# The expert stage of a decoder kernel: another order of the experts' work, two pairs of down operands, single tiles for gathered tokens and expert outputs, all subtractions on VectorE

## The chip, the core and the metric

One core of a Trainium2 chip runs the whole kernel. The metric is the device time of an execution in microseconds (us). A span is the time from the first to the last instruction of the one profiled execution.

## What is computed

One inference step of a hybrid decoder layer: 1024 prompt tokens and 32 sample tokens go through a projection, an mLSTM branch and a sliding-window attention branch, a merge, and then a mixture of experts. The part that matters here is the last:

```python
def expert(args):
    xb, e = args
    return (jax.nn.silu(xb @ w_gate_e[e]) * (xb @ w_up_e[e])) @ w_down_e[e]

ys = lax.map(expert, (xs, blk_e)).reshape(rows, d)
out = jnp.zeros((n_tok + 1, d), jnp.float32).at[row_tok].add(ys.astype(jnp.float32) * row_w[:, None])
```

There are 32 experts (`NE`), each with gate and up matrices of 1024 x 256 and a down matrix of 256 x 1024 in fp32, 1 MB each. Every one of the 1056 tokens goes to two experts of one group, so an expert sees 66 tokens on average. A block holds up to 128.

## The kernel before

Products are made in three matmuls of float32r operands: each fp32 operand is split into a high part (a copy that rounds, on ScalarE) and a low part (operand minus high part, a subtraction), and `three` (L782) adds low x high, high x low and high x high. So each weight matrix costs a 1 MB load, a ScalarE copy of 128 x 2048 and a subtraction of 128 x 2048.

The expert stage runs all 32 experts in a pipeline written out by hand; each engine has its own loop over `e`, and semaphores join them. Per expert:

- SP (L726 to L736) loads the gate, up and down matrices into five raw tiles in turn (`raw`, two of them called `stage`), in the order of `ORDER` (L537). A load waits until the low part of the matrix five places earlier has been made.
- GpSimd (L2486 to L2504) gathers the expert's rows with an indirect DMA into `xg`, two tiles in turn (`gather`, L2470), makes the low part of the up matrix (`low`, L2481), and scatters the expert's result from `yo`, two tiles in turn (`store_y`, L2476). The gather of expert e+2 waits for the transposes of expert e.
- ScalarE (L1632 to L1656) makes the high parts of the weights (`main_high`), of the transposed x (`x_high`) and of h (`h_high`), the sigmoid (`silu`), and copies the result out of PSUM (`y_out`).
- VectorE (L2328 to L2340) makes the low parts of the gate and down matrices, of x (`x_low`) and of h (`h_low`), and the hidden product (`hidden`).
- TensorE (L1274 to L1287) runs in turn: `gate_up(e)` (24 matmuls of 512 columns), the two transposes of h of expert e-1, the eight transposes of x of expert e+1, and `down(e-1)` (12 matmuls).

Gate and up operands have two sets of tiles (`GUH`, `GUL`, by parity of e). The down operand has one pair (`dh`, `dl`), so the high part of the next down matrix waits until `down` of the expert before is done. `idx` holds, for each expert, the rows to gather and the rows to write; rows beyond an expert's count point out of bounds and are skipped. A loop for experts with more than 128 rows stands behind the stage; it isn't entered with these inputs.

Ahead of the stage, routing is computed; behind it, a last stage waits for all stores (`m_end`), loads the scattered results and adds them to the residual.

Of the kernel before, what the change touches and what calls it, by code (L numbers as in the profile page):

```python
# [15 lines left out]
F32R = mybir.dt.float32r  # L16
# [7 lines left out]
D = 1024  # L24
# [47 lines left out]
def build(nc, x_prompt, x_sample, state_C, state_n, state_m, cache_k, cache_v, w_in, b_if, norm_mix,  # L72
# [28 lines left out]
    with ctx:  # L101
# [145 lines left out]
        with s4:  # L247
# [19 lines left out]
                OB = r4("OB", [128, 2 * NT, 2, NBLK])  # L267
            gu1h = a4("gu1h", [128, 2 * CHUNK], F32R)
            gu1l = a4("gu1l", [128, 2 * CHUNK], F32R)
            dh = a4("dh", [128, CHUNK], F32R)  # L270
            dl = a4("dl", [128, CHUNK], F32R)
            raw = stage + [a4(f"raw{i}", [128, CHUNK]) for i in range(2)]
            a4("padw", [128, HOLE - 8 * CHUNK])
            idx = a4("idx", [128, 2, NBLK], I32)
            wgt = a4("wgt", [128, 2, NT])
            ovt = a4("ovt", [1, 2, NOVER], I32)
# [27 lines left out]
            s4b = ExitStack()  # L304
            with s4b:
                c4 = lambda n, s, dt=F32: alloc(s4b, n, s, dt)
                xg = [c4(f"xg{i}", [128, D]) for i in range(2)]
                xh = [c4(f"xh{i}", [128, KT, 128], F32R) for i in range(2)]
                xl = [c4(f"xl{i}", [128, KT, 128], F32R) for i in range(2)]
                ixs = c4("ixs", [128, 1], I32)  # L310
                dxs = c4("dxs", [128, 1], I32)
                sg_ = c4("sg_", [128, FF])
                hh = c4("hh", [128, FF])
                hTh = c4("hTh", [128, 2, 128], F32R)
                hTl = c4("hTl", [128, 2, 128], F32R)
                yo = [c4(f"yo{i}", [128, D]) for i in range(2)]
            s4c = ExitStack()
            with s4c:
                d4 = lambda n, s, dt=F32: alloc(s4c, n, s, dt)
# [1 line left out]
        gE = raw[3][:, 0:D]  # L321

        GUH, GUL = [whi2[:, :], gu1h[:, :]], [wlo2[:, :], gu1l[:, :]]


        pb = [ctx.enter_context(nc.psum_tensor(f"pb{i}", [128, 512], F32)) for i in range(4)]
# [209 lines left out]

        ORDER = [("g", 0), ("u", 0), ("g", 1)]  # L537
        for e_ in range(NE + 1):
            ORDER += [(m, k) for m, k in (("u", e_ + 1), ("d", e_ - 1), ("g", e_ + 2)) if 0 <= k < NE
                      and (m, k) not in ORDER]  # L540
        PLACE = {c: q for q, c in enumerate(ORDER)}
        NRAW = len(raw)
        HI, LO = {"g": g_hi, "u": u_hi, "d": d_hi}, {"g": g_lo, "u": u_lo, "d": d_lo}
# [10 lines left out]
        def half(tiles, par, m):  # L554

            if m == "d":
                return tiles[2].rearrange("p (k n) -> p k n", k=2)
            return tiles[par].rearrange("p (k n) -> p k n", k=KT)[:, :, (m == "u") * FF:(1 + (m == "u")) * FF]

        WHI, WLO = GUH + [dh[:, :]], GUL + [dl[:, :]]  # L560

        R_END = 4

# [213 lines left out]
        def _(pe):  # L777
# [4 lines left out]
            def three(out, lh, ll, rh, rl, first, last):  # L782

                pe.matmul(out, ll, rh, start=first, stop=False)  # L784
                pe.matmul(out, lh, rl, start=False, stop=False)  # L785
                return pe.matmul(out, lh, rh, start=False, stop=last)  # L786
# [458 lines left out]
            def transposes_h(e):  # L1245
                pe.wait_ge(e_hh, e + 1)
                for k in range(2):
                    mm = pe.transpose(pb[0][:, k * 128:(k + 1) * 128], hh[:, k:FF:2], ident)
                mm.then_inc(e_ht, 1)
# [9 lines left out]
                               k == 0, k == KT - 1)  # L1259
                mm.then_inc(e_gu, 1)  # L1260

            def down(e):
                pe.wait_ge(e_lo, e + 1)
                pe.wait_ge(d_lo, e + 1)
                for k in range(2):
                    for n_ in range(2):
                        wsl = slice(k * D + n_ * 512, k * D + (n_ + 1) * 512)
                        mm = three(pq[:, n_, :], hTh[:, k, :], hTl[:, k, :], dh[:, wsl], dl[:, wsl], k == 0, k == 1)
                mm.then_inc(e_y, 1)

            transposes_x(0, 0, 16)
            for e in range(NE + 1):
                if e < NE:
                    if e >= 2:  # L1274
                        pe.wait_ge(e_hh, e - 1)
                    gate_up(e, e % 2)
                if e >= 1:
                    if e >= 2:
                        pe.wait_ge(e_lo, e - 1)
                    transposes_h(e - 1)  # L1280
                if e + 1 < NE:
                    pe.wait_ge(e_xl, e + 1)
                    transposes_x(e + 1, (e + 1) % 2, 16 * ((e + 1) // 2 + 1))
                if e >= 1:
                    if e >= 2:
                        pe.wait_ge(e_yc, e - 1)
                    down(e - 1)  # L1287
            any_ = pe.value_load(ovt[0:1, 0, 0:1], min_val=0, max_val=1)
            with pe.If(any_ > 0):
                with pe.Fori(0, NOVER) as j:  # L1290
                    used_ = pe.value_load(ovt[0:1, 0, bass.ds(j, 1)], min_val=0, max_val=1)
                    with pe.If(used_ > 0):
                        e = j + NE
                        pe.wait_ge(e_xl, e)
                        transposes_x(e, 0, j * 16 + 16 * (NE // 2 + 1))
                        pe.wait_ge(e_hh, e)
                        gate_up(e, 0)
                        pe.wait_ge(e_lo, e)
                        transposes_h(e)
                        pe.wait_ge(e_yc, e)  # L1300
                        down(e)
                    with pe.Else():
                        pe.nop()
            with pe.Else():
# [5 lines left out]
        def _(act):  # L1310
# [289 lines left out]
            def main_high(m, e):  # L1600
                q = PLACE[m, e]
                high(q, m, e % 2, landed(q))
# [23 lines left out]

            def y_out(e, par, stored):
                act.wait_ge(e_y, e + 1)
                act.wait_ge(st_y[par], stored)
                copy(yo[par][:, :].rearrange("p (a n) -> p a n", a=2), pq[:, :, :]).then_inc(e_yc, 1)  # L1630

            act.wait_ge(r_v, R_END)  # L1632
            x_high(0, 0)
            main_high("g", 1)
            for e in range(NE + 2):
                if e + 1 < NE:
                    if e >= 1:
                        act.wait_ge(e_gu, e)
                    main_high("u", e + 1)
                if 1 <= e <= NE:  # L1640
                    if e >= 2:
                        act.wait_ge(e_y, e - 1)
                    main_high("d", e - 1)
                if e >= 2:
                    y_out(e - 2, e % 2, 16 * ((e - 2) // 2 + 1))
                if 1 <= e <= NE:
                    h_high(e - 1)
                if e < NE:
                    if e >= 1:
                        act.wait_ge(e_hh, e)  # L1650
                    silu(e, e % 2)
                if e + 1 < NE:
                    x_high(e + 1, (e + 1) % 2)
                if e + 2 < NE:
                    act.wait_ge(e_gu, e + 1)
                    main_high("g", e + 2)  # L1656
            any_ = act.value_load(ovt[0:1, 0, 0:1], min_val=0, max_val=1)
            with act.If(any_ > 0):
                with act.Fori(0, NOVER) as j:
                    used_ = act.value_load(ovt[0:1, 0, bass.ds(j, 1)], min_val=0, max_val=1)  # L1660
                    with act.If(used_ > 0):
                        e = j + NE
                        act.wait_ge(e_gu, e)
                        act.wait_ge(e_y, e)
                        for i, m in enumerate("gud"):
                            high(i, m, 0, j * 16 + (LAST[i] + 16))
                        x_high(e, 0)
                        silu(e, 0)
                        h_high(e)
                        y_out(e, 0, j * 16 + 16 * (NE // 2 + 1))  # L1670
                    with act.Else():
                        act.nop()
            with act.Else():
# [12 lines left out]
        def _(ve):  # L1686
# [640 lines left out]

            x_low(0, 0)  # L2328
            for e in range(NE + 1):
                if e + 1 < NE:  # L2330
                    low(PLACE["g", e + 1], "g", (e + 1) % 2, e + 1)
                if e >= 1:
                    low(PLACE["d", e - 1], "d", 0, e - 1)
                    h_low(e - 1)
                if e < NE:
                    if e >= 1:
                        ve.wait_ge(e_ht, e)
                    hidden(e, e % 2)
                if e + 1 < NE:
                    x_low(e + 1, (e + 1) % 2)  # L2340
            any_ = ve.value_load(ovt[0:1, 0, 0:1], min_val=0, max_val=1)
            with ve.If(any_ > 0):
                with ve.Fori(0, NOVER) as j:
# [38 lines left out]
        def _(gp):  # L2382
# [105 lines left out]
            gp.wait_ge(r_v, R_END)  # L2488
            for i in range(2):
                gp.wait_ge(st_h[i], 16 * ((NT + 1 - i) // 2))  # L2490
            for x in xg:
                gp.memset(x[:, :], 0.0)
            gp.drain()
            gather(idx[:, 0, 0:1], 0)
            gather(idx[:, 0, 1:2], 1)
            for e in range(NE + 2):
                if e + 2 < NE:
                    gp.wait_ge(e_xt, e + 1)
                    gather(idx[:, 0, e + 2:e + 3], e % 2)
                if e + 1 < NE:  # L2500
                    low("u", e + 1)
                if e >= 2:
                    gp.wait_ge(e_yc, e - 1)
                    store_y(idx[:, 1, e - 2:e - 1], e % 2)  # L2504
# [103 lines left out]
```

## Time and profile before

| | us |
|---|---|
| median of 3 runs | 1966.74 (1950.81 to 1970.0) |
| the profiled execution's own time | 1960.17 |
| its span | 1958.4 |
| first transpose of x to landing of the last store | 1533.9 to 1912.0 |
| one period of the settled expert stage | 11.2 |

In the rows further down, PE is TensorE's matmuls, DVE is VectorE, ACT ScalarE, POOL GpSimd. A group is named by its line, engine and operation, and by the tiles it writes and reads; buffer numbers are left out. Line L1318 is the helper that ScalarE's copies share, L2305 is VectorE's weight subtraction, L2483 GpSimd's, L2472 the gather, L2477 the store. L784 to L786 are the three matmuls, L1242 the transposes of x, L1248 those of h. `gu1h`, `whi` and `gu1l`, `wlo` are the high and low gate and up operands of the two parities. What stands in brackets is the idle time just before the instruction and what ended it.

### The profile page before, as it was taken

To read this page: it belongs to the slowest core of one execution; us is meant where nothing else is said; L and a number is where in the kernel's file an instruction comes from. 1 tells how busy PE (TensorE), PEld (TensorE's weight loads), DVE (VectorE), ACT (ScalarE), POOL (GpSimd) and SP (SyncE) were. 2 spreads that over 40 slices of the span, in tenths; PEclk is the share of its full clock that TensorE was granted. 3 is DMA by queue.
4 is the path that set the end of the run, shared out by engine and by line. 5 is a ranking of instruction groups with operands and counts; after the bars stand their busy time and mean duration, and the time that the engine had idled before them with its cause. 6 is when DMAs were issued, how large, how long until landed. Compare 5 with 4: busy or idle time off the path is not lost.

```text
span 1958.4 us, 27717 instructions
## 1 busy us (share of the span) xinstructions
PE 1697.9 (87%) x11221; PEld 1539.7 (79%) x11222; DVE 911.7 (47%) x1527; ACT 695.9 (36%) x1248; POOL 429.2 (22%) x241
## 2 busy tenths in 40 slices
PE   5969899999998999999999669998993688888870
PEld 4958898998987999888888459998993577767760
DVE  5433113123122001565566352344226498998957
ACT  4312222232221221433434231322022477677642
POOL 3000101002002000000000140000022487887842
PEclk7979999999998999999999679999996799999995
DMA  5033714508417222433321253435123499999946
GB/s 182 1 108 63 123 39 90 112 22 99 125 21 130 85 88 92 138 117 106 100 75 63 105 207 88 121 99 179 39 88 114 145 325 329 333 327 334 330 149 270
DMA packets 147568, 272.16 MB, mean 139 GB/s; under 512 B 44124, under 2 KB 114076, under 8 KB 134060
## 3 DMA queue, kind: packets, MB, share of 16 engines
q1 hardware_dynamic: 111792, 210.76, 33.2%
q0 software_dynamic: 16736, 40.14, 6.4%
q10 hardware_dynamic: 18912, 19.47, 5.9%
q8 instruction: 90, 1.47, 0.4%
q14 instruction: 38, 0.31, 0.1%
HBM read 223.22 MB, written 65.38 MB: 147 GB/s over the span
## 4 chain that ended last, share of the span: by engine, by line
PE 72%; DVE 10%; ACT 6%; issue 5%; DMA 3%; DVEq 2%; POOL 1%; SPq 0%; POOLq 0%; ACTq 0%
PE pb L784 14%; PE pb L785 13%; PE pb L786 13%; PE pb L1003 8%; DVE dl L2305 4%; ACT gu1h L1318 2%; PE pw L784 2%; PE pw L785 2%; PE pw L786 2%; ACT dh L1318 2%; PE pw L1014 2%; PE pw L892 1%; PE pq L858 1%; PE pb L1025 1%; PE pq L784 1%
## 5 line engine op out<-in xcount | busy, mean ns | idle before, releaser
L784 PE MATMUL pb<-whi,aTl 128*128 128x256 f32 (+1 forms) x1296 | 377.7, 291 | 17.1 <-ACT zo L1318 8.8
L785 PE MATMUL pb<-wlo,aTh 128*128 128x256 f32 (+1 forms) x1296 | 369.1, 285 | 0.0
L786 PE MATMUL pb<-whi,aTh 128*128 128x256 f32 (+1 forms) x1296 | 366.5, 283 | 0.0
L784 PEld LDWEIGHTS pb<-whi,aTl 128*128 128x128 f32 (+1 forms) x1296 | 236.1, 182 | 28.6 <-ACT zo L1318 13.0
L784 PE MATMUL pb<-aTh,wlo 128*128 128x352 f32 x720 | 235.9, 328 | 20.6 <-DVE mixT L2067 8.7
L786 PEld LDWEIGHTS pb<-whi,aTh 128*128 128x128 f32 (+1 forms) x1296 | 237.3, 183 | 1.0
L785 PEld LDWEIGHTS pb<-wlo,aTh 128*128 128x128 f32 (+1 forms) x1296 | 236.0, 182 | 2.1
L785 PE MATMUL pb<-aTl,whi 128*128 128x352 f32 x720 | 232.7, 323 | 0.0
L786 PE MATMUL pb<-aTh,whi 128*128 128x352 f32 x720 | 232.6, 323 | 0.0
L1694 DVE TENSOR_TENSOR wlo<-stage,whi 128x2048 fp32r<-128x2048 f32 x34 | 77.8, 2288 | 225.8 <-ACT whi L1318 225.8
L1318 ACT ACTIVATE whi<-stage 128x2048 fp32r<-128x2048 f32 (+1 forms) x80 | 109.8, 1397 | 132.0 <-PEq L1203 47.7
L784 PEld LDWEIGHTS pb<-aTh,wlo 128*128 128x128 f32 x720 | 136.8, 190 | 24.9 <-issue 15.8
L785 PEld LDWEIGHTS pb<-aTl,whi 128*128 128x128 f32 x720 | 137.1, 190 | 0.0
L786 PEld LDWEIGHTS pb<-aTh,whi 128*128 128x128 f32 x720 | 136.6, 190 | 0.0
L1003 PE MATMUL pb<-aTh,wlo 128*128 128x352 f32 x384 | 126.4, 329 | 0.3 <-PE pb L786 0.3
L1003 PE MATMUL pb<-aTh,whi 128*128 128x352 f32 x384 | 126.1, 328 | 0.0
L1003 PE MATMUL pb<-aTl,whi 128*128 128x352 f32 x384 | 124.3, 324 | 0.0
L1318 ACT ACTIVATE zo<-pb 128x256 f32<-128x256 f32 (+1 forms) x90 | 34.5, 383 | 224.0 <-PE pb L786 213.4
L2305 DVE TENSOR_TENSOR dl<-raw,dh 128x2048 fp32r<-128x2048 f32 x19 | 103.2, 5434 | 21.5 <-ACT dh L1318 21.5
L2431 POOL DMA_DIRECT2D oT_scratch<-ot x16 | 12.0, 753 | 455.7 <-ACT ot L1318 455.7
L1471 ACT ACTIVATE Sm<-Sm,nmx 128x256 f32<-128x256 f32 x128 | 63.5, 497 | 114.4 <-DVE nmx L1958 114.4
L784 PE MATMUL pq<-dh,hTl 128*128 128x512 f32 x128 | 54.2, 423 | 47.7 <-DVE hTl L2325 46.7
(411 smaller groups left out, 3446.5 us busy)
## 6 DMA issues: line engine op xcount, KB each, us to landing
stage<-in_w_in SPq DMA_DIRECT2D x30, 1024.0 KB, 5.6
raw<-in_w_gate_e SPq DMA_DIRECT2D x19, 1024.0 KB, 6.8
raw<-in_w_up_e SPq DMA_DIRECT2D x19, 1024.0 KB, 8.8
raw<-in_w_down_e SPq DMA_DIRECT2D x19, 1024.0 KB, 7.8
stage<-in_w_gate_e SPq DMA_DIRECT2D x13, 1024.0 KB, 6.9
stage<-in_w_up_e SPq DMA_DIRECT2D x13, 1024.0 KB, 8.7
stage<-in_w_down_e SPq DMA_DIRECT2D x13, 1024.0 KB, 8.2
zt_scratch<-zo ACTq DMA_DIRECT2D x80, 128.0 KB, 2.4
```

Of the source, the lines that this page charges most:

```text
L784: pe.matmul(out, ll, rh, start=first, stop=False)
L785: pe.matmul(out, lh, rl, start=False, stop=False)
L786: return pe.matmul(out, lh, rh, start=False, stop=last)
L858: mm = pe.matmul(pq[0:n, 1, 0:MD + 1], qT[:, d, tok(c)], Ce[:, d, :], start=(d == 0), stop=(d == 1))
L892: mm = pe.matmul(pw[:, d, 0:MD + 1], kw[c % 2][:, d * 128:(d + 1) * 128], v1[:, c, :], start=True, stop=True)
L1003: mm = pe.matmul(ZB[f % 2][:, 0:NC], lh, rh, start=(k == 0 and m == 0), stop=(k == KT - 1 and m == 2))
L1014: mm = pe.matmul(pw[:, e, v * 256:(v + 1) * 256], qTs[lo:lo + AD, gp * 4 + 2 * (p % 2) + v, :], kTs[lo:lo + AD, gp, :], start=True, stop=True)
L1025: mm = pe.transpose(AB[v][:, (2 * e + half) * 128:(2 * e + half + 1) * 128], Sm[p % 2][:, 2 * e + v, half * 128:(half + 1) * 128], ident)
L1318: return act.activation(out, in_, ACT.Copy, scale=scale)
L1471: act.activation(x, x, ACT.Exp, bias=nmx[:, h:h + 1], accum_out=den[:, h:h + 1])
L1694: ve.tensor_tensor(wlo[sl], stage[st][:, :], whi[sl].bitcast(F32), ALU.subtract).then_inc(w_lo, 1)
L2305: ve.tensor_tensor(half(WLO, par, m), rawv(q, m), half(WHI, par, m).bitcast(F32), ALU.subtract).then_inc(LO[m], 1)
```

## The change

The diff, cut to its core (a second, unentered loop for overfull experts is adapted in the same way):

```diff
-            dh = a4("dh", [128, CHUNK], F32R)
-            dl = a4("dl", [128, CHUNK], F32R)
+            d0h = a4("d0h", [128, CHUNK], F32R)
+            d0l = a4("d0l", [128, CHUNK], F32R)
...
-            a4("padw", [128, HOLE - 8 * CHUNK])
+            sg_ = a4("sg_", [128, FF])
+            hh = a4("hh", [128, FF])
...
-                xg = [c4(f"xg{i}", [128, D]) for i in range(2)]
+                xg = [c4("xg", [128, D])] * 2
...
-                yo = [c4(f"yo{i}", [128, D]) for i in range(2)]
+                yo = [c4("yo", [128, D])] * 2
+                d1h = c4("d1h", [128, CHUNK], F32R)
+                d1l = c4("d1l", [128, CHUNK], F32R)
...
-            ORDER += [(m, k) for m, k in (("u", e_ + 1), ("d", e_ - 1), ("g", e_ + 2)) if 0 <= k < NE
-                      and (m, k) not in ORDER]
+            ORDER += [(m, k) for m, k in (("u", e_ + 1), ("d", e_), ("g", e_ + 2)) if 0 <= k < NE]
...
             for e in range(NE + 1):
+                if e + 1 < NE:
+                    pe.wait_ge(e_xl, e + 1)
+                    transposes_x(e + 1, (e + 1) % 2, 16 * ((e + 1) // 2 + 1))
                 if e < NE:
                     if e >= 2:
                         pe.wait_ge(e_hh, e - 1)
                     gate_up(e, e % 2)
                 if e >= 1:
                     if e >= 2:
-                        pe.wait_ge(e_lo, e - 1)
-                    transposes_h(e - 1)
-                if e + 1 < NE:
-                    pe.wait_ge(e_xl, e + 1)
-                    transposes_x(e + 1, (e + 1) % 2, 16 * ((e + 1) // 2 + 1))
-                if e >= 1:
-                    if e >= 2:
                         pe.wait_ge(e_yc, e - 1)
-                    down(e - 1)
+                    down(e - 1, (e - 1) % 2)
+                if e < NE:
+                    if e >= 1:
+                        pe.wait_ge(e_lo, e)
+                    transposes_h(e)
...
                 act.wait_ge(e_y, e + 1)
-                act.wait_ge(st_y[par], stored)
+                act.wait_ge(st_y[1 - par], stored)
...
             for e in range(NE + 2):
+                if 1 <= e <= NE:
+                    if e >= 2:
+                        act.wait_ge(e_y, e - 1)
+                    h_high(e - 1)
+                if e >= 2:
+                    y_out(e - 2, e % 2, 16 * ((e - 1) // 2 + 1))
                 if e + 1 < NE:
                     if e >= 1:
                         act.wait_ge(e_gu, e)
+                    x_high(e + 1, (e + 1) % 2)
                     main_high("u", e + 1)
-                if 1 <= e <= NE:
-                    if e >= 2:
-                        act.wait_ge(e_y, e - 1)
-                    main_high("d", e - 1)
-                if e >= 2:
-                    y_out(e - 2, e % 2, 16 * ((e - 2) // 2 + 1))
-                if 1 <= e <= NE:
-                    h_high(e - 1)
                 if e < NE:
+                    main_high("d", e)
                     if e >= 1:
                         act.wait_ge(e_hh, e)
                     silu(e, e % 2)
-                if e + 1 < NE:
-                    x_high(e + 1, (e + 1) % 2)
                 if e + 2 < NE:
-                    act.wait_ge(e_gu, e + 1)
                     main_high("g", e + 2)
...
             for e in range(NE + 1):
+                if e >= 1:
+                    h_low(e - 1)
                 if e + 1 < NE:
                     low(PLACE["g", e + 1], "g", (e + 1) % 2, e + 1)
-                if e >= 1:
-                    low(PLACE["d", e - 1], "d", 0, e - 1)
-                    h_low(e - 1)
+                    x_low(e + 1, (e + 1) % 2)
+                    low(PLACE["u", e + 1], "u", (e + 1) % 2, e + 1)
                 if e < NE:
                     if e >= 1:
                         ve.wait_ge(e_ht, e)
                     hidden(e, e % 2)
-                if e + 1 < NE:
-                    x_low(e + 1, (e + 1) % 2)
+                    low(PLACE["d", e], "d", e % 2, e)
...
-            for x in xg:
-                gp.memset(x[:, :], 0.0)
+            gp.memset(xg[0][:, :], 0.0)
             gp.drain()
             gather(idx[:, 0, 0:1], 0)
-            gather(idx[:, 0, 1:2], 1)
             for e in range(NE + 2):
-                if e + 2 < NE:
+                if e + 1 < NE:
                     gp.wait_ge(e_xt, e + 1)
-                    gather(idx[:, 0, e + 2:e + 3], e % 2)
-                if e + 1 < NE:
-                    low("u", e + 1)
+                    gather(idx[:, 0, e + 1:e + 2], (e + 1) % 2)
                 if e >= 2:
                     gp.wait_ge(e_yc, e - 1)
                     store_y(idx[:, 1, e - 2:e - 1], e % 2)
```

There are now two down pairs, `d0h`, `d0l` and `d1h`, `d1l`, used by parity of e. `xg` and `yo` are one tile each: the gather of expert e+1 waits for the transposes of expert e, and `y_out` of an expert waits until the store of the expert before has landed. TensorE's order per expert is: transposes of x of e+1, `gate_up(e)`, `down(e-1)`, transposes of h of e. GpSimd makes no weight subtraction inside the loop (those of expert 0's gate and up stay with it); VectorE makes all three of each later expert. `sg_` and `hh` move into a gap of the layout.

## Rows read from the trace of the kernel before

**Rows 1.** Engine busy us (instructions), granted clock, DMA share, GB/s, in two periods

```profile
1560.00:1571.20 11.20, 9.79 (x47) 7.99 (x46) 10.17 (x8) 8.01 (x9) 8.35 (x3) 1.00 0.86 307
...
1582.40:1593.60 11.20, 9.79 (x47) 7.98 (x46) 10.10 (x8) 8.06 (x9) 9.12 (x4) 1.00 0.94 327
```

**Rows 2.** Waits of the expert stage: us in total, times, longest us

```profile
PE pq L784 <- DVE hTl L2325: 45.3, 30, 4.5
```

**Rows 3.** Timeline of VectorE and GpSimd, one period: start, us, instruction, idle before it

```profile
1696.80 5.20 POOL L2483 TENSOR_TENSOR gu1l<-raw,gu1h 128x2048 fp32r<-128x2048 f32 x1 [1.65 <-ACT gu1h L1318]
...
1698.55 5.60 DVE L2305 TENSOR_TENSOR dl<-stage,dh 128x2048 fp32r<-128x2048 f32 x1 [1.03 <-ACT dh L1318]
...
1702.16 2.87 POOL L2477 DMA_INDIRECT ys_scratch<-yo,idx  x1 [0.16 <-issue]
...
1705.34 1.00 POOL L2472 DMA_INDIRECT xg<-h_scratch,idx  x1 [0.31 <-issue]
...
1706.42 2.28 DVE L2305 TENSOR_TENSOR wlo<-stage,whi 128x2048 fp32r<-128x2048 f32 x1
```

**Rows 4.** The same timeline, TensorE and ScalarE, the half period behind it

```profile
1704.58 0.48 PE L784 MATMUL pq<-dh,hTl 128*128 128x512 f32 x1 [1.41 <-DVE hTl L2325]
...
1707.46 0.40 PE L784 MATMUL pw<-gu1h,xl 128*128 128x512 f32 x1
...
1713.09 0.39 PE L1248 MATMUL pb<-cst,hh 128*128 128x128 f32 x2
...
1713.31 1.06 PE L1242 MATMUL pb<-cst,xg 128*128 128x128 f32 x8
...
1713.51 0.38 ACT L1318 ACTIVATE hTh<-pb 128x256 fp32r<-128x256 f32 x1 [2.90 <-PE pb L1248]
...
1714.41 1.09 ACT L1318 ACTIVATE xh<-pb 128x512 fp32r<-128x512 f32 x2 [0.24 <-PE pb L1242]
...
1715.38 1.92 ACT L1318 ACTIVATE gu1h<-raw 128x2048 fp32r<-128x2048 f32 x1
```

**Rows 5.** Timeline and one clock window, where the expert stage starts

```profile
1523.97 1.84 POOL L2492 MEMSET xg<- 128x1024 f32 x2 [31.45 <-DVEq L2299]
...
1533.87 1.94 PE L1242 MATMUL pb<-cst,xg 128*128 128x128 f32 x8 [10.67 <-DMA xg<-h_scratch,idx]
...
1547.51 1.01 POOL L2472 DMA_INDIRECT xg<-h_scratch,idx  x1 [1.93 <-PE pb L1242]
...
1549.23 0.80 PE L784 MATMUL pw<-gu1h,xl 128*128 128x512 f32 x1 [2.50 <-DVE xl L2318]
...
1549.00:1550.00 1.00, 0.77 (x2) 0.67 (x3) 0.49 (x2) 1.00 (x2) 0.00 (x0) 0.50 0.86 308
```

**Rows 6.** Timeline of GpSimd, the first store and the gather behind it

```profile
1567.81 2.88 POOL L2477 DMA_INDIRECT ys_scratch<-yo,idx  x1 [0.17 <-issue]
...
1571.00 1.03 POOL L2472 DMA_INDIRECT xg<-h_scratch,idx  x1 [0.31 <-issue]
```

**Rows 7.** DMA view: gathers issued at 1529, 1558, 1571.0 and 1705.3, us to landing

```profile
xg<-h_scratch,idx POOLq DMA_INDIRECT x1, 4.3
...
xg<-h_scratch,idx POOLq DMA_INDIRECT x1, 6.6
...
xg<-h_scratch,idx POOLq DMA_INDIRECT x1, 8.9
...
xg<-h_scratch,idx POOLq DMA_INDIRECT x1, 11.7
```

**Rows 8.** Timelines and chain of waits, where the expert stage ends

```profile
1896.40 0.39 PE L1248 MATMUL pb<-cst,hh 128*128 128x128 f32 x2
...
1906.76 1.02 ACT L1318 ACTIVATE yo<-pq 128x1024 f32<-128x1024 f32 x1 [7.07 <-PE pq L786]
...
1908.56 0.97 POOL L2477 DMA_INDIRECT ys_scratch<-yo,idx  x1 [6.88 <-ACT yo L1318]
...
1908.56 3.39 DMA ys_scratch<-yo,idx
```

More of the change, by code:

```diff
@@ L269, in build @@
             gu1l = a4("gu1l", [128, 2 * CHUNK], F32R)
-            dh = a4("dh", [128, CHUNK], F32R)
-            dl = a4("dl", [128, CHUNK], F32R)
+            d0h = a4("d0h", [128, CHUNK], F32R)
+            d0l = a4("d0l", [128, CHUNK], F32R)
             raw = stage + [a4(f"raw{i}", [128, CHUNK]) for i in range(2)]
-            a4("padw", [128, HOLE - 8 * CHUNK])
+            sg_ = a4("sg_", [128, FF])
+            hh = a4("hh", [128, FF])
+            assert 2 * FF + 8 * CHUNK == HOLE
             idx = a4("idx", [128, 2, NBLK], I32)
@@ L311, in build @@
                 dxs = c4("dxs", [128, 1], I32)
-                sg_ = c4("sg_", [128, FF])
-                hh = c4("hh", [128, FF])
                 hTh = c4("hTh", [128, 2, 128], F32R)
                 hTl = c4("hTl", [128, 2, 128], F32R)
-                yo = [c4(f"yo{i}", [128, D]) for i in range(2)]
+                yo = [c4("yo", [128, D])] * 2
+                d1h = c4("d1h", [128, CHUNK], F32R)
+                d1l = c4("d1l", [128, CHUNK], F32R)
             s4c = ExitStack()
@@ L323, in build @@
         GUH, GUL = [whi2[:, :], gu1h[:, :]], [wlo2[:, :], gu1l[:, :]]
+        DH, DL = [d0h[:, :], d1h[:, :]], [d0l[:, :], d1l[:, :]]
         pb = [ctx.enter_context(nc.psum_tensor(f"pb{i}", [128, 512], F32)) for i in range(4)]
@@ L556, in half @@
             if m == "d":
-                return tiles[2].rearrange("p (k n) -> p k n", k=2)
+                return tiles[2 + par].rearrange("p (k n) -> p k n", k=2)
             return tiles[par].rearrange("p (k n) -> p k n", k=KT)[:, :, (m == "u") * FF:(1 + (m == "u")) * FF]
-        WHI, WLO = GUH + [dh[:, :]], GUL + [dl[:, :]]
+        WHI, WLO = GUH + DH, GUL + DL
         R_END = 4
@@ L1260, in gate_up, with down @@
                 mm.then_inc(e_gu, 1)
-            def down(e):
+            def down(e, par):
                 pe.wait_ge(e_lo, e + 1)
@@ L1267, in down @@
                         wsl = slice(k * D + n_ * 512, k * D + (n_ + 1) * 512)
-                        mm = three(pq[:, n_, :], hTh[:, k, :], hTl[:, k, :], dh[:, wsl], dl[:, wsl], k == 0, k == 1)
+                        mm = three(pq[:, n_, :], hTh[:, k, :], hTl[:, k, :], DH[par][:, wsl], DL[par][:, wsl],
+                                   k == 0, k == 1)
                 mm.then_inc(e_y, 1)
@@ L1300, in _ @@
                         pe.wait_ge(e_yc, e)
-                        down(e)
+                        down(e, 0)
                     with pe.Else():
@@ L1669, in _ @@
                         h_high(e)
-                        y_out(e, 0, j * 16 + 16 * (NE // 2 + 1))
+                        act.wait_ge(st_y[0], j * 16 + 16 * (NE // 2 + 1))
+                        y_out(e, 0, 16 * (NE // 2 + 1))
                     with act.Else():
```

## The prediction, made blind

> **What bounds it now.** Read the busy table by period first: in a settled 11.2 us period of the expert stage (one expert, 32 in all) VectorE is busy 10.1 us, TensorE 9.8, GpSimd 9.1, ScalarE 8.1, the clock is at its upper level (1.00, 2.4 GHz) and the DMA engines are busy 0.94 of the time at 327 GB/s [rows 1]. Everything is nearly full, so the waits decide. TensorE waits 1.5 us per expert for `hTl` on VectorE [rows 2]. The timeline shows why `hTl` is late: the down subtraction takes 5.60 us, but the same subtraction takes 2.28 us when GpSimd is idle [rows 3]. It ends 2.15 us after GpSimd's own 5.20 us subtraction ends (1696.80 + 5.20 = 1702.00; 1698.55 + 5.60 = 1704.15), so it stood still for 3.3 us until GpSimd was done. VectorE with that standstill is the loop that sets 11.2 us.
>
> The same rows show a second thing: GpSimd's store issue began at 1702.16 and ended at 1705.03, 0.88 us after VectorE's subtraction, where an undisturbed one takes 0.97 [rows 3, 8]. An indirect DMA issue, too, stands behind a VectorE subtraction that is running.
>
> A rule of the Trainium skill (SBUF — State Buffer, Who interferes with whom) fits the first: two SBUF inputs on VectorE and a reading GpSimd instruction exclude each other, first come first served. But it also holds that tensor_tensor was not seen to stall a DMA issued by GpSimd; these rows show that it does. By the rule the store in the sum below would be through 0.7 us earlier (12.0 + 0.97 against 13.7), and the sum would come out 10 us lower (14 x 0.7).
>
> **The change, part by part.** *All subtractions on VectorE.* VectorE loses 3.3 us of standstill and gains 2.28: 10.1 - 3.3 + 2.3 = 9.1 us. GpSimd keeps only DMA issues. *Two pairs of down operands, new order.* The down operand is ready before it is needed, and the wait of [rows 2] goes; what is late next is dealt with below. TensorE's own sequence is transposes of x 0.90 (1.06 less the overlap of a last matmul), gate and up 5.63 (1707.46 to 1713.09, 24 matmuls, so 0.235 each), down 12 x 0.235 = 2.82, transposes of h 0.22: 9.6 us [rows 4]. By the engines alone the period could fall to 9.6. The bytes are the same: 0.94 x 11.2 = 10.5 us at a full DMA share [rows 1]. SP's loads come in another order, but each still goes out five places ahead; I cost that at nothing.
>
> *One tile each for x and y.* This is the price. Before, the gather for expert e+2 goes out after the transposes of e and has two periods. Now it goes out only after the transposes of e+1, and on GpSimd it stands behind the store of expert e-2, which waits for `y_out`. So a chain runs from the transposes of expert e to those of e+2, two periods long. Its terms, from the start of the transposes of e:
>
> 0.90 + 5.63 + 2.82 and 0.42 until ScalarE copies h: 9.8. The copy 0.38 [rows 4]: 10.15. `y_out` 1.02 and 0.78 of hand-over to GpSimd [rows 8]: the store is issued at 12.0. VectorE meanwhile: `h_low` (about as long as its high part, 0.4), then the gate subtraction 2.28, until 12.8. The store stands behind it, and its descriptors are out 0.88 later, at **13.7**. The gather follows by 0.3. By then x is free (transposes of e+1 end at P + 0.9, plus 0.8), where P is the period.
>
> From the end of the store's issue to the landing of the gather behind it the trace gives two ends. In the settled stage 1705.34 + 11.7 - 1705.03 = 12.0 us; for the first store 1571.00 + 8.9 - 1570.69 = 9.2 us [rows 3, 6, 7]. I take **9.2**: with a period over 12 us the DMA share falls to 10.5 / 12.1 = 0.87, about that of the period in which the first store goes out (0.86 [rows 1]), and the gather before has landed before each store goes out. A gather with no store ahead landed in 6.6 among loads, in 4.3 on a quiet chip [rows 7]. Landing to the first transpose: 0.2.
>
> *Clock.* TensorE now idles before the transposes of x. Uneven spacing follows from the start (9.6, then the rest), so every second gap is about 3 us. A gap of 2.50 us left the clock at 0.50 (1.2 GHz) [rows 5]. At that level the transposes take 1.94 instead of 1.06 [rows 4, 5], and the first gate matmuls some 0.3 more: **1.2** in one of two periods. If short gaps save the clock, it is 0.
>
> Two periods: 13.7 + 9.2 + 0.2 + 1.2 = **24.3**, so P = 12.15 against 11.2.
>
> *Start.* One memset less, half of 1.84: the transposes of expert 0 start at 1533.87 - 0.92 = 1532.95 [rows 5]. They take 1.94, then 0.8, gather 4.3, 0.2: expert 1 at 1540.2. Transposes 1.9, gate and up 5.6 with 0.8 for the low clock, sigmoid and hidden 1.3: expert 2 at 1550.0, expert 3 at 1559.6. *Middle.* Expert 30: 1550.0 + 14 x 24.3 = 1890.2; expert 31, 9.6 + 1.2 later: 1901.0. *End.* From there 0.90 + 2 x (5.63 + 2.82) + 0.22 + 0.42 = 18.4 to the copy of the last h: 1919.4 (before: 1896.40 + 0.42 [rows 8]). Then copy 0.4, `y_out` of expert 30 1.0, its store 0.8 + 3.4, `y_out` of 31 1.0, its store 0.8 + 3.4: 10.8, and the last store lands at 1930.2. Before it lands at 1908.56 + 3.39 = 1911.95 [rows 8]. The stages ahead and behind are untouched. Sum: **+18 us**, 1960.2 to 1978 in the profiled execution's own time. That execution is 6.6 below the median of the three runs; the middle of all four is 1963.5, and on that I set 1982.
>
> **Rivals.** (A is the forecast; times on 1963.5.)
>
> *B: the queue stays as full as now.* Gather 12.0 after the store: two periods 27.1, expert 30 at 1929.4, end at 1969.4, +57; without the clock loss +39. 2003 to 2021. For it: 30 settled periods show it. Against it: a longer period carries the same bytes.
>
> *C, faster: the queue drains.* If the gather lands under 7.8 us after the store's issue, P is under 10.8 and the kernel is more than 1% faster; the floor is the full DMA share, P = 10.5: expert 31 at 1559.6 + 28 x 10.5 = 1853.6, end 29.2 later at 1882.8, -29: 1934. For it: 6.6 for a lone gather. Against it: no store and gather pair among loads took under 9.2 in the rows above.
>
> *D: the period does not move.* The loads themselves, at 0.94 busy, hold 11.2: end at 1559.6 + 28 x 11.2 + 29.2 = 1902.4, -10 from start and end alone: 1954. For it: the share of [rows 1]. Against it: it needs 8.5 in the queue.
>
> **How the numbers follow.** A 0.50, between 0 (no clock loss: two periods 23.1, expert 31 at 1883.0, end at 1912.2) and +33 (a gather at 10.3), so 1964 to 1997 by itself. B 0.22, C 0.16, D 0.12. A measurement of this kernel tells about 1% (20 us) from no change. C is faster: 0.16. D and nearly half of A are within 1%: 0.36. B and the rest of A are slower: 0.48. The range leaves out about 0.1 at either side, the lower half of C and the upper half of B: 1942 to 2010.
>
> **What would show it.** Right: `hTl` no longer heads TensorE's waits; every VectorE subtraction of 128x2048 takes 2.3 us; TensorE's largest wait is the transposes of x on the DMA of `xg`; the store's issue is longer than 1 us; periods alternate, with windows of clock under 1.00 behind the long gaps. Wrong: TensorE waiting for VectorE or for loads, periods of 10 to 11 us, or gathers landing within 5 us of their issue.

## The result and the profile after

| | before | after |
|---|---|---|
| median | 1962.66 us (4 runs, 1950.81 to 1970.0) | 1996.97 us (4 runs, 1989.33 to 2002.64) |
| the profiled execution's own time | 1960.17 | 1998.1 |
| landing of the last store in it | 1911.95 | 1949.1 |

The ratio is 1.0178, with a 95% interval from 1.0113 to 1.0243: the change makes the kernel 34 us slower. The forecast was 1982, so the sign and the range held, and the added time came out near twice the predicted 18 us. The stages ahead of and behind the expert stage did not move: the last store lands 37.1 us later, and the profiled execution is 37.9 us longer.

First the waits of the kernel after, over the settled expert stage (1560 to 1935): engine, line and what it waited for, us in total, times, longest.

```profile
POOL ys_scratch L2478 <- ACT yo L1321: 209.8, 29, 10.8
...
PE pb L1244 <- DMA xg<-h_scratch,idx: 62.3, 14, 5.2
...
ACT yo L1321 <- DMA ys_scratch<-yo,idx: 0.7, 2, 0.5
```

The wait for `hTl` of [rows 2] is gone. In its place TensorE waits for the gather, in every second period, 4.45 us on average. GpSimd stands 7.2 us per expert (209.8 / 29) in front of a store until ScalarE has copied y, and the gather is queued behind that store. ScalarE hardly ever waits for the single y tile.

Next the timeline of the kernel after over two experts, TensorE, ScalarE, VectorE and GpSimd in order of time: start, us, engine, line, instruction, and in brackets the idle time before it and what ended it.

```profile
1702.56 1.94 PE L1244 MATMUL pb<-cst,xg 128*128 128x128 f32 x8 [4.19 <-DMA xg<-h_scratch,idx]
...
1704.15 0.78 PE L786 MATMUL pw<-gu1h,xl 128*128 128x512 f32 x1
...
1711.74 0.40 PE L786 MATMUL pq<-d0h,hTl 128*128 128x512 f32 x1
...
1714.53 0.39 PE L1250 MATMUL pb<-cst,hh 128*128 128x128 f32 x2
1714.76 1.06 PE L1244 MATMUL pb<-cst,xg 128*128 128x128 f32 x8
...
1715.30 1.02 ACT L1321 ACTIVATE yo<-pq 128x1024 f32<-128x1024 f32 x1
...
1715.86 2.28 DVE L2306 TENSOR_TENSOR gu1l<-raw,gu1h 128x2048 fp32r<-128x2048 f32 x1
...
1717.12 1.91 POOL L2478 DMA_INDIRECT ys_scratch<-yo,idx  x1 [10.82 <-ACT yo L1321]
...
1719.25 2.29 DVE L2306 TENSOR_TENSOR gu1l<-stage,gu1h 128x2048 fp32r<-128x2048 f32 x1
1719.33 3.10 POOL L2473 DMA_INDIRECT xg<-h_scratch,idx  x1 [0.31 <-issue]
...
1721.28 0.39 PE L786 MATMUL pq<-d1h,hTl 128*128 128x512 f32 x1
...
1728.74 1.94 PE L1244 MATMUL pb<-cst,xg 128*128 128x128 f32 x8 [4.32 <-DMA xg<-h_scratch,idx]
```

Read it from top to bottom as the chain of the prediction: transposes of x, gate and up, down, the transposes of h, ScalarE's copy of y, the store, the gather behind it, the next but one transposes of x. The subtractions take 2.28 to 2.29 us: the standstill of [rows 3] is gone. But the store's issue meets the gate subtraction, takes 1.91 us and ends 0.89 us after it (1715.86 + 2.28 = 1718.14; 1717.12 + 1.91 = 1719.03). The gather's issue meets the up subtraction, takes 3.10 us and ends 0.89 us after that. Expert e+1 (1714.76) has its x in time; expert e+2 (1728.74) has not, and that repeats: the gaps between transposes are some 12 and 14 us in turn.

The DMA view of the kernel after, us from issue to landing: the gather issued at 1705.27, 2.77 us after the issue of the store ahead of it had ended, and the one at 1719.33, 0.31 us after.

```profile
xg<-h_scratch,idx POOLq DMA_INDIRECT x1, 6.1
...
xg<-h_scratch,idx POOLq DMA_INDIRECT x1, 9.3
```

The busy table of the kernel after by stretch: length, busy us and instructions of PE, PEld, DVE, ACT and POOL, granted clock, DMA share, GB/s; first two half pairs, then single microseconds behind the long gap.

```profile
1700.00:1713.00 13.00, 10.44 (x38) 8.69 (x39) 5.65 (x6) 5.69 (x6) 2.94 (x2) 0.74 0.81 293
1713.00:1726.00 13.00, 11.42 (x56) 9.33 (x54) 12.44 (x12) 10.67 (x11) 5.01 (x2) 1.00 0.76 280
...
1707.00:1708.00 1.00, 1.00 (x4) 0.81 (x3) 0.49 (x2) 1.00 (x2) 0.00 (x0) 0.50 0.71 267
1708.00:1709.00 1.00, 1.00 (x5) 0.77 (x5) 1.00 (x1) 1.00 (x1) 0.00 (x0) 0.84 0.55 217
1709.00:1710.00 1.00, 1.00 (x6) 0.82 (x5) 0.81 (x1) 0.29 (x1) 0.00 (x0) 1.00 0.37 152
```

In [rows 1] the DMA engines were busy 0.86 to 0.94 of the time at 307 to 327 GB/s; now 0.76 to 0.81 at 280 to 293. The chip has become less full, and the kernel slower. Behind the gap of 4.19 us TensorE works at 0.50 (1.2 GHz) until into the window at 1708, some 6 us, not only through the transposes.

### The profile page after: what moved, and what is told of

Same layout as the page of the kernel before. It is cut to its first block, busy times and chain, and to the rows that moved or that the text cites. A ratio compares the mean times of both kernels' runs of the same rounds, so it can differ in the third digit from the quotient of the medians.

```text
span 1996.3 us, 27686 instructions
## 1 busy us (share of the span) xinstructions
PE 1717.5 (86%) x11221; PEld 1560.3 (78%) x11222; DVE 884.1 (44%) x1558; ACT 699.0 (35%) x1248; POOL 266.3 (13%) x209
## 4 chain that ended last, share of the span: by engine, by line
PE 73%; DMA 10%; DVE 6%; issue 5%; ACT 2%; POOL 2%; DVEq 1%; SPq 1%; POOLq 0%; ACTq 0%
PE pb L786 14%; PE pb L787 13%; PE pb L788 13%; PE pb L1005 8%; DMA xg<-h_scratch,idx 7%; PE pw L786 2%; PE pw L787 2%; PE pw L788 2%; PE pb L1244 2%; PE pw L1016 1%; PE pw L894 1%; PE pq L860 1%; POOL ys_scratch L2478 1%; PE pb L1027 1%; DMA zt_scratch<-zo 1%
## 5 line engine op out<-in xcount | busy, mean ns | idle before, releaser
L786 PE MATMUL pb<-whi,aTl 128*128 128x256 f32 (+1 forms) x1296 | 377.1, 291 | 20.3 <-ACT zo L1321 10.7
L786 PEld LDWEIGHTS pb<-whi,aTl 128*128 128x128 f32 (+1 forms) x1296 | 235.7, 182 | 31.8 <-ACT zo L1321 14.9
L786 PEld LDWEIGHTS pb<-aTh,wlo 128*128 128x128 f32 x720 | 137.3, 191 | 18.9 <-issue 15.0
L1244 PE MATMUL pb<-cst,xg 128*128 128x128 f32 x256 | 48.0, 349 | 77.2 <-DMA xg<-h_scratch,idx 77.2
L1244 PEld LDWEIGHTS pb<-cst,xg 128*128 128x128 f32 x256 | 40.8, 207 | 79.9 <-issue 79.9
L2478 POOL DMA_INDIRECT ys_scratch<-yo,idx x32 | 56.4, 1763 | 233.1 <-ACT yo L1321 222.2
```

Of the source, the lines that this page charges most:

```text
L1244: mm = pe.transpose(TB[0][k // 4][:, (k % 4) * 128:(k % 4 + 1) * 128], xg[par][:, k:D:KT], ident)
L2478: gp.indirect_dma_start(out=ys_d, out_offset=bass.IndirectOffsetOnAxis(ap=index, axis=0), in_=yo[par][:, :], in_offset=None, bounds_check= ...
```

## The experiments

All were timed beside the kernel before, on one chip for each batch: first `two_x`, `two_y`, `gather_first` and `warm` (before: 1957.3), then the other four (before: 1957.02). Differences in us between kernels are worked out from their ratios, times 1957. `two_y` runs like the changed kernel (1.0186 beside 1.0178) and stands for it in the first batch.

**Undo one tile at a time.** `two_x` gives the gather its second tile back (it lies in columns of the constants' tile that this stage doesn't use) with its old place in the order; everything else is the changed kernel.

```diff
-                xg = [c4("xg", [128, D])] * 2
+                xg = [c4("xg", [128, D]), cst[:, 128:128 + D]]
...
             gather(idx[:, 0, 0:1], 0)
+            gather(idx[:, 0, 1:2], 1)
             for e in range(NE + 2):
-                if e + 1 < NE:
+                if e + 2 < NE:
                     gp.wait_ge(e_xt, e + 1)
-                    gather(idx[:, 0, e + 1:e + 2], (e + 1) % 2)
+                    gather(idx[:, 0, e + 2:e + 3], e % 2)
```

> The changed kernel with a second x tile again (in columns of the constants that nothing reads any more), so that the gather of expert e+2 goes out after the transposes of e. My theory (the chain transposes of e, store of e-2, gather of e+2, transposes of e+2 sets 25.6 us per two experts): TensorE no longer waits for the gather, the clock stays up, a period is 10 to 11 us, and the time falls from 1997 by 30 to 50 us. Rival, the single y tile sets the pace (the copy of a result waits for the store before it): no change, 1987 to 2007. Rival, three subtractions on VectorE are too many: no change either.

Measured: 1918.93 us (1911.77 to 1925.91), a ratio to before of 0.9791 [0.9747, 0.9835]. `two_y` does the same for the y tile, and `y_out` waits for the store two experts back again:

```diff
-                yo = [c4("yo", [128, D])] * 2
+                yo = [c4("yo", [128, D]), cst[:, 128:128 + D]]
...
-                act.wait_ge(st_y[1 - par], stored)
+                act.wait_ge(st_y[par], stored)
...
-                    y_out(e - 2, e % 2, 16 * ((e - 1) // 2 + 1))
+                    y_out(e - 2, e % 2, 16 * ((e - 2) // 2 + 1))
```

> The changed kernel with a second y tile again and one x tile. My theory: the wait of the copy on the store before is 0.7 us in the whole stage, so the time stays within 10 us of 1997. Rival (y tile): it falls by more than 25 us.

Measured: 1996.16 us, 1.0186 [1.0154, 1.0218], the time of the changed kernel; `two_x` is (1.0186 - 0.9791) x 1957 = 77 us under it. So the whole loss, and a gain hidden under it, hang on the x tile; the y tile costs nothing beside a single x tile. The DMA view of `two_x` for a gather issued at 1676.00, and its busy table over 40 us:

```profile
xg<-h_scratch,idx POOLq DMA_INDIRECT x1, 10.6
```

```profile
1600.00:1640.00 40.00, 38.34 (x183) 30.89 (x182) 35.67 (x33) 32.24 (x32) 8.20 (x8) 1.00 0.98 366
```

The gather takes longer here, 10.6 us, than the 9.3 that stalled the changed kernel. It has two periods for it, TensorE no longer waits for it, the clock stays at 1.00, and the period falls to about 10.1 us.

**What stands ahead of the gather.** `gather_first` keeps the single x tile, and has GpSimd issue the gather of e+1 before the store that stood ahead of it (the store goes one turn later).

```diff
-            for e in range(NE + 2):
+            for e in range(NE + 3):
...
-                if e >= 2:
-                    gp.wait_ge(e_yc, e - 1)
-                    store_y(idx[:, 1, e - 2:e - 1], e % 2)
+                if e >= 3:
+                    gp.wait_ge(e_yc, e - 2)
+                    store_y(idx[:, 1, e - 3:e - 2], (e - 3) % 2)
```

> The changed kernel with one x and one y tile, but on GpSimd each store is issued behind the next gather instead of ahead of it. My theory: the gather then waits only for the transposes before it (0.8 us of hand-over, 1.0 of issue, 4 to 5 to land), the two-period chain is gone, and the period becomes 10 to 11 us: 30 to 50 us less than 1997. Rival (y tile): the store leaves later, so the copy of the next result waits for it, the period is 12 us or more, and the time is 1990 or higher. Rival (the gather is slow by itself, not by what stands ahead of it): no change.

Measured: 1937.52 us (1933.53 to 1940.58), 0.9896 [0.9863, 0.9929], 57 us under the changed kernel: faster than before with one tile. Its timeline, TensorE and GpSimd, and the DMA view of the gather in it:

```profile
1679.71 1.13 PE L1244 MATMUL pb<-cst,xg 128*128 128x128 f32 x8 [1.21 <-DMA xg<-h_scratch,idx]
...
1681.61 1.02 POOL L2473 DMA_INDIRECT xg<-h_scratch,idx  x1 [8.62 <-PE pb L1244]
1684.20 1.01 POOL L2478 DMA_INDIRECT ys_scratch<-yo,idx  x1 [1.57 <-ACT yo L1321]
...
1690.03 1.13 PE L1244 MATMUL pb<-cst,xg 128*128 128x128 f32 x8
```

```profile
xg<-h_scratch,idx POOLq DMA_INDIRECT x1, 8.3
```

The loop of a single x tile without the store is there to read: transposes at 1679.71, gather issued 1.90 later, landing 8.3 us after that, next transposes at 1690.03: 10.3 us, close to the 10.1 of `two_x`. So it is the tile and the queue together: of the 77 us that the tile costs, 57 come from the store, with its wait for ScalarE, standing ahead of the gather in GpSimd's loop.

**The clock's share.** `warm` lets TensorE transpose the identity 30 times, into a PSUM bank that nothing reads, in each long gap.

```diff
                 if e + 1 < NE:
+                    if e >= 3 and e % 2 == 1:
+                        for _ in range(30):
+                            pe.transpose(pb[1][:, 0:128], ident, ident)
                     pe.wait_ge(e_xl, e + 1)
```

> The changed kernel with 30 transposes of the identity into an unused PSUM bank ahead of every second expert's transposes of x, in the long gaps, so that TensorE doesn't idle there. My theory: the transposes and the first gate products behind the gap run at the upper clock, the chain loses up to 2.6 us per two periods, and the time falls by 15 to 35 us. If the low clock is only a symptom and hidden behind the gather: no change (1987 to 2007), or slower by what the 30 transposes (3.5 us) overrun the gap.

Measured: 1973.64 us (1968.51 to 1983.64), 1.0091 [1.0059, 1.0123], 19 us under the changed kernel. Its timeline, the transposes of x behind two long gaps:

```profile
1694.22 1.13 PE L1244 MATMUL pb<-cst,xg 128*128 128x128 f32 x8 [0.98 <-DMA xg<-h_scratch,idx]
...
1717.79 1.13 PE L1244 MATMUL pb<-cst,xg 128*128 128x128 f32 x8 [1.02 <-DMA xg<-h_scratch,idx]
```

They take 1.13 instead of 1.94, and this pair takes 23.57 us instead of 25.64 in the mean of the changed kernel, with the gather as late as ever behind its store. Seven of 13 pairs take 23.4 to 23.6. In the six others, 24.6 to 26.7, the gather lands 10.3 to 10.8 us after its issue instead of 9.2, and behind two of them TensorE still loses 1.5 us (11.1 to 11.2 us from these transposes to the next, elsewhere 9.6); the mean is 24.4. So some 19 of the 77 us are the clock's, a consequence of the gap. `gather_first` shortens the gap too, to 1.21 us in the rows above, so these 19 are not to be added to its 57.

**One part alone, on the kernel before.** `old_one_x` only takes away its second x tile; `old_all_ve` only moves the up subtraction to VectorE.

```diff
-                xg = [c4(f"xg{i}", [128, D]) for i in range(2)]
+                xg = [c4("xg", [128, D])] * 2
...
-            gather(idx[:, 0, 1:2], 1)
             for e in range(NE + 2):
-                if e + 2 < NE:
+                if e + 1 < NE:
                     gp.wait_ge(e_xt, e + 1)
-                    gather(idx[:, 0, e + 2:e + 3], e % 2)
+                    gather(idx[:, 0, e + 1:e + 2], (e + 1) % 2)
```

> The kernel before, with the single x tile of the change alone: the gather of expert e+1 waits for the transposes of e, and goes out ahead of GpSimd's up subtraction and the store. My theory: in the old order too the gather is then late. From the end of the transposes 0.8 of hand-over, 1.0 of issue and 6 to 10 us to land, next to the 1 us of the transposes: a period of 11.5 to 13 us against 11.2, so 10 to 60 us slower than the kernel before. Rival (only the new order makes the single tile costly): within 10 us of it.

Measured: 1986.6 us (1983.23 to 1998.57), 1.0151 [1.0109, 1.0193], 30 us slower.

```diff
                     low(PLACE["g", e + 1], "g", (e + 1) % 2, e + 1)
+                    low(PLACE["u", e + 1], "u", (e + 1) % 2, e + 1)
...
-                if e + 1 < NE:
-                    low("u", e + 1)
```

> The kernel before, with the subtraction of the up matrices moved from GpSimd to VectorE and nothing else. My theory (VectorE loses 3.3 us of standstill per expert and takes on 2.3): the period falls from 11.2 by 0.5 to 1.2 us, 15 to 40 us faster than the kernel before. Rival (the single down pair and the order hold the period by themselves): no change.

Measured: 1925.04 us (1918.88 to 1929.09), 0.9823 [0.9787, 0.9859], 35 us faster. The waits of `old_one_x`, of `old_all_ve` and of the kernel before, all over 1560 to 1850:

```profile
PE pb L1242 <- DMA xg<-h_scratch,idx: 27.4, 14, 3.8
```

```profile
PE pq L784 <- DVE hTl L2325: 6.4, 19, 0.7
```

```profile
PE pq L784 <- DVE hTl L2325: 35.2, 25, 1.5
```

And the busy table of `old_all_ve` over 40 us, with two transposes of x in a row from its timeline:

```profile
1600.00:1640.00 40.00, 39.40 (x188) 32.22 (x187) 36.54 (x33) 32.26 (x32) 13.51 (x9) 1.00 0.98 372
...
1610.20 1.06 PE L1242 MATMUL pb<-cst,xg 128*128 128x128 f32 x8
...
1620.06 1.06 PE L1242 MATMUL pb<-cst,xg 128*128 128x128 f32 x8
```

Three things follow. Moving the subtraction alone takes the wait of [rows 2] from 35.2 us in this stretch to 6.4 and is worth 35 us, with one pair of down operands and the old order. What holds `old_all_ve` in these 40 us is TensorE's own sequence: it is busy 39.40 of them, and from 1610.20 to 1620.06 it has no idle time that the timeline shows, 9.86 us for an expert. The DMA share of 0.98 that stands beside it doesn't show that the transfers set the period. Later they do count: from 1700 to 1850 ScalarE waits for loads of down matrices, 11.5 us in all, and from 1800 to 1840 TensorE is busy only 38.31 us. The interval of `two_x`, which has the second pair and the new order besides, overlaps that of `old_all_ve`; but `two_x` is held by its y tile (below), so what those two parts are worth by themselves no run shows.

And with a single x tile, the old order (1.0151) and the changed kernel (1.0178) end within their intervals of each other. In both the chain that ended last runs through the gather into the one tile; in `old_one_x` it runs on through GpSimd's up subtraction ahead of the store, in the changed kernel through TensorE and the y copy. Nothing in the rows makes the two chains equally long.

**What bounds `two_x`.** In it ScalarE's y copy still waits for the store before, 56.0 us in all over 1560 to 1850, ahead of the copies that feed the next expert. `two_x_late_y` puts `y_out` behind them.

```diff
-                if e >= 2:
-                    y_out(e - 2, e % 2, 16 * ((e - 1) // 2 + 1))
                 if e + 1 < NE:
...
                     main_high("u", e + 1)
+                if e >= 2:
+                    y_out(e - 2, e % 2, 16 * ((e - 1) // 2 + 1))
```

> The run with two x tiles, and ScalarE copies the result out behind the x and up copies instead of ahead of them. There ScalarE waits 2.0 us per expert for the store before. My theory: the wait goes, and the period falls from 10.1 towards TensorE's 9.6: 5 to 15 us less than 1919. Rival (the DMA engines, 0.97 busy there, hold 10.1): no change within 5 us.

Measured: 1924.12 us (1920.84 to 1928.83), 0.9823 [0.979, 0.9856], no gain; the DMA share is 0.96 to 1.00. My expectation fell, but the run doesn't clear the wait: it is still there, 45.6 us over the same stretch.

```profile
ACT yo L1321 <- DMA ys_scratch<-yo,idx: 45.6, 28, 2.5
```

The chain that ended last says why, in `two_x` first, then in `two_x_late_y`: start, us, what.

```profile
1633.34 8.54 DMA ys_scratch<-yo,idx
...
1641.97 1.04 ACT yo L1321
...
1643.79 8.56 DMA ys_scratch<-yo,idx
...
1652.43 1.04 ACT yo L1321
```

```profile
1632.61 8.27 DMA ys_scratch<-yo,idx
...
1640.96 1.04 ACT yo L1321
...
1642.78 8.68 DMA ys_scratch<-yo,idx
```

It is a ring through the single y tile: the store lands 8.5 us after its issue, the next result is copied into the tile (1.03), 0.8 later its store is issued. From 1603.01 to 1847.25 `two_x` issues 24 stores behind the first, 10.18 us each, and between 1600 and 1840 the chain holds nothing else. Moving the copy to another place in ScalarE's loop leaves the ring as it is. So with the second x tile given back, the y tile sets the pace. The full DMA engines enter by the landing, 8.5 us where the last store of the kernel before took 3.39 [rows 8]; no engine of `two_x` waits for a load of weights in that stretch, so the rival, that the loads hold the period, isn't borne out. Two x tiles and two y tiles together, in the new order, were not run.

**The standstill by itself, and a miss.** `two_x_pool_u` is `two_x` with the up subtraction back on GpSimd, ahead of the store in its loop.

```diff
-                    low(PLACE["u", e + 1], "u", (e + 1) % 2, e + 1)
...
                     gather(idx[:, 0, e + 2:e + 3], e % 2)
+                if e + 1 < NE:
+                    low("u", e + 1)
                 if e >= 2:
```

> The run with two x tiles, with the subtraction of the up matrices back on GpSimd: this takes back one part of the change. My theory (the two engines shut each other out when both subtract): a VectorE subtraction takes up to 5.5 us again, the stores leave late, and the period is 11 to 12.5 us: 30 to 75 us slower than 1919. Rival (the second down pair and the order take the subtractions out of the way anyhow): within 15 us of 1919.

Measured: 2163.96 us (2157.57 to 2171.8), 1.1047 [1.1006, 1.1089]: 246 us above `two_x`, where I had put at most 75. Its timeline, ScalarE, GpSimd and VectorE:

```profile
1605.23 1.02 ACT L1321 ACTIVATE yo<-pq 128x1024 f32<-128x1024 f32 x1 [10.77 <-DMA ys_scratch<-yo,idx]
...
1607.11 1.92 ACT L1321 ACTIVATE whi<-raw 128x2048 fp32r<-128x2048 f32 x1
...
1609.11 4.58 POOL L2483 TENSOR_TENSOR wlo<-raw,whi 128x2048 fp32r<-128x2048 f32 x1 [8.66 <-ACT whi L1321]
...
1612.04 3.80 DVE L2306 TENSOR_TENSOR d1l<-raw,d1h 128x2048 fp32r<-128x2048 f32 x1
...
1613.85 2.87 POOL L2477 DMA_INDIRECT ys_scratch<-yo,idx  x1 [0.16 <-PE pb L1244]
...
1624.13 1.02 ACT L1321 ACTIVATE yo<-pq 128x1024 f32<-128x1024 f32 x1 [10.90 <-DMA ys_scratch<-yo,idx]
```

The standstill is there (3.80 us instead of 2.28), but it is a small part. The rows close a ring of 18.9 us: the y copy (1605.23), behind it the up copy (1607.11), then GpSimd's up subtraction (1609.11), behind that the store (1613.85), and the next y copy, which needs the one y tile, stands until that store has landed (1624.13). So the single y tile, free in the changed kernel, sets the pace in `two_x` with a ring of 10.2 us, and a subtraction that waits for ScalarE, ahead of the store, draws that ring out to 18.9. I had priced only the standstill. That a second y tile would open the ring was not run.

## Why the prediction was right, and where its size was off

*The mechanism held.* All five signs that it named are in the trace: `hTl` gone, subtractions at 2.28 to 2.29 us, TensorE's largest wait on its other engines and transfers the gather, a store issue over 1 us, alternating periods with a lower clock behind the long gap. `two_x` and `gather_first` show that the chain through the single tile and the queue is the cause, by undoing one link each. The time alone would not have told it: B without the clock loss, 2003, lies nearer to 1997 than A's 1982. The rows below decide between them.

*The start held.* Transposes of experts 1, 2 and 3 were forecast at 1540.2, 1550.0 and 1559.6; they came at 1539.54, 1550.27 and 1559.83.

*The pair was mis-sized, 25.64 us against 24.3.* Two rows of the kernel after, 13 pairs apart (timeline; expert 4 and expert 30):

```profile
1574.25 1.94 PE L1244 MATMUL pb<-cst,xg 128*128 128x128 f32 x8 [4.76 <-DMA xg<-h_scratch,idx]
...
1907.58 1.94 PE L1244 MATMUL pb<-cst,xg 128*128 128x128 f32 x8 [4.25 <-DMA xg<-h_scratch,idx]
```

(1907.58 - 1574.25) / 13 = 25.64. Over these pairs the first piece, from the transposes to the end of the store's issue, takes 15.82 us on average (forecast 13.7 + 1.2 = 14.9), the second, from there to the next but one transposes, 9.82 (forecast 9.2 + 0.2 = 9.4).

- The clock term is the larger miss. I took 1.2 us: the slower transposes and a little of the first gate matmuls. From the transposes to the first down matmul the timeline above shows 9.18 us behind a gap (1702.56 to 1711.74) and 6.52 without one (1714.76 to 1721.28): 2.66 us lost. Over the 13 pairs the loss is 1.3 to 2.66, on average 2.0. In the pair shown the lower level outlasts the transposes by some four microseconds and reaches far into gate and up. `warm`, whose undisturbed pairs are 2.1 us shorter, agrees. The miss is 0.8 a pair. The gaps themselves were 4.2 to 5.2 us against the forecast's 3; but the loss doesn't follow their length (a gap of 4.19 cost 2.66, one of 4.20 only 1.65), and what sets it stays open.
- The queue term was good: the second piece took 9.6 to 9.8 in eleven pairs and 10.6 in two; the miss is 0.4. I had the gather follow the store undisturbed, where its own issue met the second subtraction and took 3.10 us. Why so little of these 2.1 us shows in the landing was not tested apart.
- The rest of the first piece is 0.1 longer.

1.34 a pair is 17.4 us over the 13 pairs. The start and the first pair nearly cancel (expert 4 at 1574.25, forecast 1550.0 + 24.3 = 1574.3), and expert 31 follows expert 30 after 12.1 us instead of 10.8, so it comes at 1919.67 instead of 1901.0. From there the forecast end held (last store down at 1949.1, forecast 1930.2 + 18.7 = 1948.9). That is the whole difference between +18 and +37.

*The rivals.* B (the queue stays at 12.0) fell: none of the 13 pairs took over 10.7. C, the drained queue, and D, loads that hold 11.2, fell for the changed kernel, but their prices were wrong too. I took 10.5 us as the shortest period that the bytes allow, from a share of 0.94. `old_all_ve` moves an expert in 10.0 us at a share of 0.98 and 372 GB/s, 45 GB/s above [rows 1]. So the transfers did not set the period of before, and 0.94 was no measure of how far it could fall: with the standstill gone it came down to TensorE's own sequence, and only late in the stage to waits for loads.

*VectorE.* The step on its subtractions (standstill of 3.3 gone, 2.28 gained) was right, and `old_all_ve` gives its worth when nothing is late behind it. What the prediction left out is that this gain, 35 us, was in the change, and that the price of the single tile was set against it: 77 us, not 34.

The rule that the prediction weighed, from the Trainium skill (SBUF — State Buffer, Who interferes with whom), that tensor_tensor was not seen to stall a DMA issued by GpSimd, doesn't hold in this trace: in the rows above both issues end 0.89 us after the subtraction they met. Its other sentence, that a DMA which seems to be stalled by VectorE is one whose descriptors GpSimd writes, fits. What part of the issue is held (it also reads its row numbers from `idx`) no run separates.

The Trainium skill (Trainium Kernel Development and Optimization, Best Practices) advises double-buffering to overlap DMA with compute. `two_x` agrees for x, with 77 us; `two_y` shows nothing to be had for y as long as x has one tile; in `two_x` the ring through y sets the pace.

## What to carry to other kernels

Before a second buffer is given up, follow the whole loop through the single one: the transfer, what stands ahead of it in its issuing queue, and what that waits for; if the loop is longer than the period, the buffer sets the time, and putting the refill ahead of other work in the queue can win most of it back. Price a wait on TensorE with the slower matmuls behind it, from rows on both clock levels, and not with the gap alone. When a change has several parts, time them alone, and trace again after each: here one part was worth 35 us, another cost 77, and a third, the single y tile, cost nothing until the second was undone, and then set the pace.

The lowest time is that of `two_x`, the changed kernel with two x tiles: 2.1% [1.65%, 2.53%] under the kernel before. Its interval overlaps those of `old_all_ve` and `two_x_late_y`, so it is not shown to be better than they are.

## What the hardware showed that I had not expected

- After a gap of 4.2 us TensorE stayed at 0.50 (1.2 GHz) for about 6 us of transposes and dense matmuls in the pair shown; I had seen the fall in [rows 5], but had not priced the matmuls behind it.
- An indirect DMA issue on GpSimd takes 1.0 us alone and up to 3.1 us when it starts while a VectorE subtraction with two SBUF inputs is running. It then ends 0.89 us after it, almost the length of an undisturbed issue. An issue that starts first is not held: in `two_x` the gather at 1645.11 took 1.02 us, though a subtraction began 0.69 later.
- How long a gather's issue takes hardly shows in its landing: in `gather_first` one with an issue of 1.02 us landed 8.3 us after the start of its issue (1681.61), the next, with 3.03, after 8.1 (1691.93).
- The DMA engines reached 372 GB/s at a share of 0.98 in `old_all_ve`, where the share of 0.94 before had looked nearly full at 327.
